# Mixer norm: root applied behind the input projections, squares summed on VectorE, first slabs dealt in another order

## The reference, cut to what matters

```python
x = _layernorm(DN_ALPHA * x + y, ssd_ln_g[j], ssd_ln_b[j])   # "ln2" in the kernel
h = x
a = rmsnorm(h, g_mix[i])                  # h * rsqrt(mean(h*h) + 1e-6) * g_mix; "mix" in the kernel
proj = a @ w_in[i]
cb, cc, cu, q, k, v = jnp.split(proj, splits, axis=-1)       # 512 columns each
conv_out = head_rmsnorm(short_gated_conv(cb, cc, cu, conv_w[i]), g_conv_out[i])   # cb * conv3(cc * cu)
attn = stick_breaking_attention(to_heads(q), to_heads(k), to_heads(v))            # 8 heads of 64
attn = head_rmsnorm(attn..., g_attn_out[i])
h = h + jnp.concatenate([conv_out, attn], axis=-1) @ w_out[i]
```

## Time and profile before

| | |
|---|---|
| median of three runs | 2727.25 us |
| the profiled execution | 2722.69 us |
| its span | 2720.9 us |
| TensorE (PE) busy | 2642.7 us, 97% |
| VectorE (DVE) busy | 1713.4 us, 63% |
| ScalarE (ACT) busy | 938.1 us, 34% |
| GpSimd (POOL) busy | 1150.4 us, 42% |
| from ln2's root to the first v turned | 1372.7 to 1433.0 us |
| the attention loop | about 1436 to 1865 us |

### The profile page before, as it was taken

The page is one execution under the profiler, slowest core; times in us unless marked ns, Lnnn a source line. Parts: engine busy times, 40 slices in busy tenths (PEclk is TensorE's granted clock), DMA queues, the critical chain, the costliest instruction groups (busy, mean ns, idle before and its releaser), DMA issues.

```text
span 2720.9 us, 32191 instructions
## 1 busy us (share of the span) xinstructions
PE 2642.7 (97%) x12394; PEld 2117.3 (78%) x12394; DVE 1713.4 (63%) x2087; ACT 938.1 (34%) x1208; POOL 1150.4 (42%) x1422
## 2 busy tenths in 40 slices
PE   8999999999999999999999999998999999999998
PEld 7877878787887887887767777776888888888886
DVE  6636663778658658758865665666355656555556
ACT  2537880422212211212256666575211111111132
POOL 4633435431431431431421222223555676655653
PEclk9999999999999999999999999999999999999999
DMA  3110003210110110110230000002111111111312
GB/s 135 51 47 32 24 20 109 66 47 24 39 48 23 40 54 16 47 47 16 78 131 24 32 24 32 24 32 85 55 39 55 55 55 55 47 47 54 117 47 78
DMA packets 39937, 139.37 MB, mean 51 GB/s; under 512 B 4400, under 2 KB 4528, under 8 KB 39792
## 3 DMA queue, kind: packets, MB, share of 16 engines
q1 hardware_dynamic: 31392, 110.11, 12.3%
q10 hardware_dynamic: 8400, 27.26, 2.7%
HBM read 124.77 MB, written 12.58 MB: 50 GB/s over the span
## 4 chain that ended last, share of the span: by engine, by line
PE 82%; DVE 11%; ACT 4%; issue 2%; POOL 1%; ACTq 0%; DVEq 0%; POOLq 0%
PE PS L759 37%; PE PS L1437 13%; PE PS L1463 10%; PE PS L996 2%; PE PS L1089 2%; PE PS L1485 2%; PE PS L1130 2%; PE PS L1315 1%; PE PS L895 1%; PE PS L1332 1%; PE PS L909 1%; PE PS L1354 1%; PE PS L1132 1%; PE PS L1036 1%; ACT mla_p L1662 1%
## 5 line engine op out<-in xcount | busy, mean ns | idle before, releaser
L612 POOL CAST w_hi<-w_stage 128x1024 fp32r<-128x1024 f32 x130 | 143.3, 1102 | 1116.7 <-PE PS L759 757.9
L615 POOL TENSOR_TENSOR w_lo<-w_stage,w_hi 128x256 fp32r<-128x256 f32 x520 | 504.2, 1000 | 10.4
L759 PE MATMUL PS<-XH,w_hi 128*128 128x512 f32 x1216 | 384.6, 398 | 7.7 <-DVE XL L2519 2.9
L759 PE MATMUL PS<-XL,w_hi 128*128 128x512 f32 x1216 | 375.9, 390 | 0.0
L759 PE MATMUL PS<-XH,w_lo 128*128 128x512 f32 x1216 | 375.4, 390 | 0.0
L759 PEld LDWEIGHTS PS<-XH,w_hi 128*128 128x128 f32 x1216 | 222.4, 188 | 61.0 <-issue 10.0
L759 PEld LDWEIGHTS PS<-XL,w_hi 128*128 128x128 f32 x1216 | 228.4, 188 | 48.5
L759 PEld LDWEIGHTS PS<-XH,w_lo 128*128 128x128 f32 x1216 | 228.4, 188 | 48.4
L686 POOL TENSOR_TENSOR w_lo<-w_stage,w_hi 128x256 fp32r<-128x256 f32 x260 | 220.3, 854 | 0.0
L682 POOL CAST w_hi<-w_stage 128x256 fp32r<-128x256 f32 x260 | 125.9, 487 | 185.7 <-PE PS L1437 108.3
L1437 PE MATMUL PS<-raw_hi,w_hi 128*128 128x512 f32 x512 | 158.2, 390 | 0.0
(11 more groups left out here) (459 smaller groups left out, 5620.7 us busy)
## 6 DMA issues: line engine op xcount, KB each, us to landing
w_stage<-w SPq DMA_DIRECT2D x202, 512.0 KB, 3.3
H<-x_t ACTq DMA_DIRECT2D x8, 512.0 KB, 8.0
pj_kept<-ple_proj_tiles ACTq DMA_DIRECT2D x8, 512.0 KB, 2.6
h_kept<-H ACTq DMA_DIRECT2D x8, 512.0 KB, 3.5
H<-h_kept ACTq DMA_DIRECT2D x4, 1024.0 KB, 5.0
out_t<-out_tiles SPq DMA_DIRECT2D x16, 256.0 KB, 2.1
x_again<-x_t ACTq DMA_DIRECT2D x12, 256.0 KB, 3.1
ple_proj_a<-pj_kept ACTq DMA_DIRECT2D x1, 2048.0 KB, 9.1
```

The lines of the kernel that those rows point to most:

```text
L612: nc.gpsimd.tensor_copy(w_hi[:, slot, :, :], w_stage[:, slot, :, :]).then_inc(s_w_hi, 1)
L615: nc.gpsimd.tensor_tensor(w_lo[:, slot, k:k + 2, :], w_stage[:, slot, k:k + 2, :], w_hi[:, slot, k:k + 2, :].bitcast(F32), ALU.subtract).t ...
L759: mm = nc.tensor.matmul(outs[:, half, :], wt[:, slot, k, :], a[:, k - first, half * HB:(half + 1) * HB], start=(k == whole[0] and wt is w_ ...
```

## The change

- Mixer norm. ScalarE squares tile k into one of eight buffers of its own (MIX_SQ). It makes XH directly from H with the gain as scale, without the root. VectorE makes XL from H with a `scalar_tensor_tensor`. Scale, shift and low part are interleaved in one pass (`norm_two`). Behind the last low part VectorE adds up the eight squares (seven adds into ACM), and TensorE multiplies the ones matrix with that sum alone, in the middle of slab k.
- The root RM (per token, along the free axis, the same in all partitions) and its square RM2 are made behind the first slabs. `key_roots` also makes RK, the root per token along the partitions, by a product with the identity and a reduce.
- Where the root goes in: z is copied out as z * RK * RM; the exponential weights are multiplied by RK in the high copy (scale) and in the low part; cc * cu is multiplied by RM2 ahead of the first tap; the conv result by RM after the last tap. The output of v needs RK only, hence the weights carry it.
- The order of pieces: projection pieces 6 and 7 come directly after pieces 4 and 5; slabs v and q are dealt by the list MIX_PIECES, then four tiles of k, the ones product, four tiles of k. Slab 2 (k) also starts on its high weights.

```diff
+MIX_PIECES = [0, 0, 1, 0, 1, 0, 1, 0, 0, 1, 0, 0, 1, 1, 1, 1]
...
             proj_piece(5)
-            norm_sums(mix)
             proj_piece(6)
...
-                    if i < 2:
+                    if i < 3:
                         pe.wait_ge(s_w_hi, n + 1)
...
-            for k in range(8):
-                sb_piece(0, k)
-                if 1 <= k <= 5:
-                    sb_piece(1, k - 1)
-            progress[0] = 13
-            sb_pieces(11)
+            done = [0, 0]
+            for i in MIX_PIECES:
+                sb_piece(i, done[i])
+                done[i] += 1
+            progress[0] = 16
+            sb_pieces(4)
+            mix["ss"].wait(pe, KT - 1)
+            for half in range(2):
+                mm = nc.tensor.matmul(PS[:, 2 + half, :], CN[:, C_ONES, :], ACM[:, half * HB:(half + 1) * HB], start=True, stop=True)
+            mm.then_inc(mix["cs"].sem, 1)
+            sb_pieces(4)
+            mix["v"].wait(pe, 1)
             turn_v(0)
...
-                nc.scalar.activation(SQN[:, k % 2, :], TN[:, k % 2, :], ACT.Square, bias=col("ln2_b", k)).then_inc(mix["sq"].sem, 1)
-                if k in (0, 1):
+                nc.scalar.activation(MIX_SQ[k][:, :], TN[:, k % 2, :], ACT.Square, bias=col("ln2_b", k)).then_inc(mix["sq"].sem, 1)
+                if k < 4:
                     proj_copy(4 + k)
+                ln2["h"].wait(act, k + 1)
+                nc.scalar.activation(XH[:, k, :], H[:, k, :], ACT.Copy, scale=col("g_mix", k)).then_inc(mix["hi"].sem, 1)
+                act.dma_start(h_kept[k, :, :], H[:, k, :]).then_inc(s_hk, 16)
+                if k < 4:
                     proj_out(4 + k)
-            norm_root(mix, EPS6)
-            for k in range(KT):
-                norm_hi(mix, k)
...
+            sb_copies(SB_ORDER[0])
+            sb_copies(SB_ORDER[1])
+            nc.scalar.preload_act_table_set("natural_log_exp_and_others")
+            mix["cs"].wait(act, 1)
+            inverse_root(RM[:, :], flat(1), D, EPS6, mix["v"].sem, mix["v"].base, mix["rs"].sem)
+            sb_copies(SB_ORDER[2])
...
-                        nc.scalar.activation(WH[:, T1 % 2, :, q1:HB], a, ACT.Copy).then_inc(s_wh, 1)
+                        j1 = SB_UNITS[step - 1][1]
+                        nc.scalar.activation(WH[:, T1 % 2, :, q1:HB], a, ACT.Copy, scale=RK[:, j1:j1 + 1]).then_inc(s_wh, 1)
...
+                def low(k):
+                    mix["hi"].wait(dve, k + 1)
+                    v.scalar_tensor_tensor(out=XL[:, k, :], in0=H[:, k, :], scalar=col("g_mix", k), in1=XH_f[:, k, :],
+                                           op0=ALU.mult, op1=ALU.subtract).then_inc(mix["lo"].sem, 1)
...
                 for k in range(KT):
                     if k >= 2:
+                        ln2["h"].wait(dve, k - 1)
+                        mix["sq"].wait(dve, k - 1)
+                    v.scalar_tensor_tensor(out=TN[:, k % 2, :], in0=H[:, k, :], scalar=col("ln2_g", k), in1=RS[:, :],
+                                           op0=ALU.mult, op1=ALU.mult).then_inc(ln2["t"].sem, 1)
                     if k:
+                        shifted(k - 1)
+                    if k > 1:
+                        low(k - 2)
+                shifted(KT - 1)
+                low(KT - 2)
+                low(KT - 1)
+                for k in range(1, KT):
+                    mix["sq"].wait(dve, k + 1)
+                    if k > 1:
+                        mix["ss"].wait(dve, k - 1)
+                    v.tensor_tensor(ACM[:, :], MIX_SQ[0][:, :] if k == 1 else ACM[:, :], MIX_SQ[k][:, :], ALU.add).then_inc(mix["ss"].sem, 1)
+
+            def key_roots():
+                mix["rs"].wait(dve, 1)
+                turned = ACM[:, :].rearrange("p (j t) -> p j t", t=P)
+                v.tensor_tensor(turned, RM[:, :].rearrange("p (j t) -> p j t", t=P),
+                                CN[:, C_ID, :].unsqueeze(1).to_broadcast([P, KT, P]), ALU.mult).then_inc(mix["t"].sem, 1)
+                mix["t"].wait(dve, 1)
+                v.tensor_reduce(RK, turned, AX.X, ALU.add).then_inc(mix["t"].sem, 1)
+                mix["t"].wait(dve, 2)
+                v.tensor_tensor(RM2[:, :], RM[:, :], RM[:, :], ALU.mult).then_inc(mix["c"].sem, 1)
...
+                    v.tensor_tensor(CC[:, :], CC[:, :], RM2[:, :], ALU.mult).then_inc(mix["c"].sem, 1)
+                    mix["c"].wait(dve, root_product("cc", m))
                     cc(v.tensor_scalar(y, CC[:, :], col("c2_w", 8 + m), None, ALU.mult))
...
+                    if d == 2:
+                        v.tensor_tensor(y, y, RM[:, :], ALU.mult).then_inc(mix["c"].sem, 1)
...
-                v.tensor_tensor(WL[:, T % 3, :, q0:HB], ZS[:, T % 3, :, q0:HB], WH[:, T % 2, :, q0:HB].bitcast(F32),
-                                ALU.subtract).then_inc(s_wl, 1)
+                v.scalar_tensor_tensor(out=WL[:, T % 3, :, q0:HB], in0=ZS[:, T % 3, :, q0:HB], scalar=RK[:, j:j + 1],
+                                       in1=WH[:, T % 2, :, q0:HB].bitcast(F32), op0=ALU.mult, op1=ALU.subtract).then_inc(s_wl, 1)
...
             sb_lows(("q", 0))
+            key_roots()
             sb_lows(("k", 0))
...
-                        v.tensor_copy(z, PS[:, 0:2, q0:HB]).then_inc(s_zc, 1)
+                        v.scalar_tensor_tensor(out=z, in0=PS[:, 0:2, q0:HB], scalar=RK[:, j:j + 1],
+                                               in1=RM[:, hf * HB + q0:(hf + 1) * HB].unsqueeze(1).to_broadcast([P, 2, HB - q0]),
+                                               op0=ALU.mult, op1=ALU.mult).then_inc(s_zc, 1)
```

More of the change, by code:

```diff
@@ L91, in sb_bank_turn, with cc_step, root_product @@
     return SB_BANK_USE.index(key)
+CC_STEPS = []
+for _m in range(4):
+    for _step in range(SB_STEPS):
+        _cbs = [("cb", k[1], None) for k in sb_finished(_m, _step, 0) if k[0] == "cb"]
+        _taps = [("tap", _m, d) for d in range(3) if _step > d and ("cu", _m) in sb_finished(_m, _step - d - 1, 0)]
+        CC_STEPS += _cbs + _taps if (_m, _step) in HEAD_STEPS else _taps + _cbs
+        CC_STEPS += [("cb", k[1], None) for k in sb_finished(_m, _step, 1) if k[0] == "cb"]
+def cc_step(kind, m, d=None):
+    return CC_STEPS.index((kind, m, d)) + 1
+ROOT_PRODUCTS = ["root"] + [(kind, m) for m in range(4) for kind in ("cc", "y")]
+def root_product(*key):
+    return ROOT_PRODUCTS.index(key) + 1
+MIX_PIECES = [0, 0, 1, 0, 1, 0, 1, 0, 0, 1, 0, 0, 1, 1, 1, 1]
 DT_STEPS = 23
@@ L1289, in sb_piece @@
                         pe.wait_ge(s_bank, sb_bank_turn((kind, m)))
-                mm = product(outs, n, XH, XL, [k], 0, range(8), ready=(mix["lo"].sem, mix["lo"].base) if i == 0 else None, quarters=i < 2)
+                mm = product(outs, n, XH, XL, [k], 0, range(8), ready=(mix["lo"].sem, mix["lo"].base) if i == 0 else None, quarters=i < 3)
                 if k == 7:
@@ L2504, in _, with norm_two @@
             half_low(1, KT - 1)
-            def norm_dve(s, gain, center=None, split=True, keep=False):
-                t = Tally(dve, s["t"].sem, s["t"].base)
-                if center:
-                    c = center
-                    s["cs"].wait(dve, 1)
-                    c(v.tensor_scalar(MU[:, :], flat(2), 1.0 / D, None, ALU.mult)); c.wait()
-                    for k in range(KT):
-                        c(v.tensor_tensor(H[:, k, :], H[:, k, :], MU[:, :], ALU.subtract))
-                s["rs"].wait(dve, 1)
+            def norm_two(c):
+                ln2["cs"].wait(dve, 1)
+                c(v.tensor_scalar(MU[:, :], flat(2), 1.0 / D, None, ALU.mult)); c.wait()
+                for k in range(KT):
+                    c(v.tensor_tensor(H[:, k, :], H[:, k, :], MU[:, :], ALU.subtract))
+                ln2["rs"].wait(dve, 1)
@@ L2521, in shifted @@
                 def shifted(k):
-                    s["t"].wait(dve, k + 1)
-                    v.tensor_scalar(H[:, k, :], TN[:, k % 2, :], col("ln2_b", k), None, ALU.add).then_inc(s["h"].sem, 1)
-                finish = low if split else shifted
+                    ln2["t"].wait(dve, k + 1)
+                    v.tensor_scalar(H[:, k, :], TN[:, k % 2, :], col("ln2_b", k), None, ALU.add).then_inc(ln2["h"].sem, 1)
                 for k in range(KT):
                     if k >= 2:
-                        s["lo" if split else "h"].wait(dve, k - 1)
-                        if not split:
-                            mix["sq"].wait(dve, k - 1)
-                    t(v.scalar_tensor_tensor(out=TN[:, k % 2, :], in0=H[:, k, :], scalar=col(gain, k), in1=RS[:, :],
-                                             op0=ALU.mult, op1=ALU.mult))
-                    if k:
-                        finish(k - 1)
@@ L2788, in _ @@
             out_tiles(N_CORE + 3, GROUPS - 1, centre2)
-            norm_dve(ln2, "ln2_g", center=centre2, split=False, keep=True)
-            norm_dve(mix, "g_mix")
+            norm_two(centre2)
             cc = Tally(dve, s_cc)
```

30 lines of the change are left out of this document (15 added, 15 removed).

## The result

The changed kernel took 2729.8 us (median of its runs) against 2724.45 for the kernel before beside it: a ratio of 1.0016, 95% interval 1.0009 to 1.0022. It is slower, by less than 0.2%, where 0.9975 was forecast. One run of each kernel took twice as long (5567 and 5333 us) and is left out of the ratio. The profiled execution took 2726.88 us with a span of 2725.1.

A forecast was written before the change was run, and what follows sets the result against it. TensorE, busy 97% of the span, was taken as the bound. Front -12.2 us plus loop +5.4 us made -6.8 us: 2715.9 against the profiled execution, 2720.4 us carried over to the median; range 2714 to 2730.

The forecast's parts named there:

- GpSimd's split of slab q: Second norm: cast 1.30 us, low parts 6.60 us; VectorE loses 2.5 us over five instructions beside it.
- the front: Stretch from second norm's root through slab k: k ends at 1420.6 instead of 1432.9, gain 12.2 us.
- TensorE is held by GpSimd's weights: Rival: the front keeps its end, so only the loop's +5.4 us shows, 2732.6 us; chance 0.05.
- The Trainium skill's rule: Splits in the front: VectorE would lose 3.9 us a split, not 2.5; net would be -4.2 us.
- the clock stays at the upper level: Front: TensorE's clock keeps 2.4 GHz through the stretch with waits, as from 1376 to 1404 before.
- the loop cost: Attention loop, 1436 to 1865: 20.6 us added to VectorE and ScalarE together, of which 5.4 us shows.
- VectorE's front: Second norm: scale, shift and low part take 3.23 us a tile; last low part ends at 1401.1.
- The adds: Seven adds of squares end at 1412.8, TensorE wants the sum at 1413.4: no wait, margin 0.6 us.
- VectorE's front queue longer: Rival: contention or late high parts make TensorE wait for the sum; net +0.2, 2727.4 us; chance 0.22.
- the shares named for "faster": Chance 0.56 of measurably faster: two thirds of forecast's cases, nearly all of loop hides, a fifth of long front queue.
- Passing on: Loop: 18 TensorE waits on softplus low parts and low weights pass on the added VectorE and ScalarE time, 2.0 us.
- Products: Loop, two new products per head pair: exposed 1.0 us in pair 0, 0.3 in pairs 1 and 2, 2.1 in last.

The follow-up runs named there:

- e5: The changed kernel unaltered, run again in a later session; 2719.0 us, ratio 0.9973.
- e12: e10's kernel with VectorE waiting for its own low part once, at k = 6; 2724.3 us, ratio 0.9992.
- first trace: Trace of the changed kernel's profiled execution in its first measurement, against the kernel before; 2726.88 us.
- e13: e10's kernel with all eight v tiles ahead of q; 2722.1 us, ratio 0.9991.
- e10: The changed kernel with projection piece 7 moved behind the first v tile; 2729.3 us, ratio 1.0016.
- e4: The changed kernel without the eight convolution products with the root and its square; 2715.8 us, ratio 0.9964.
- e8: The changed kernel unaltered once more, on one chip with the kernel with gaps; 2718.8 us, ratio 0.9976.
- the first study: First measurement of the changed kernel beside the kernel before; 2729.8 us, ratio 1.0016.
- e2: The changed kernel with VectorE waiting for its own low part at k = 4 alone; 2718.9 us, ratio 0.9974.
- e6: The changed kernel with the column root left out of the weights' high and low parts; 2714.8 us, ratio 0.9958.
- e7: The changed kernel with z copied plainly, without both roots; 2716.1 us, ratio 0.9963.
- the late variants: The changed kernel with projection piece 7 behind the first v tile (e10 to e13) or the second (e14); 2719.8 to 2729.3 us.
- The kernel with gaps: The changed kernel with e1's waits, run in two sessions; 2719.5 and 2718.7 us, ratio 0.9978 both times.
- e11: e10's kernel with VectorE waiting for its own low part in every tile; 2719.8 us, ratio 0.9976.
- e14: The changed kernel with projection piece 7 behind the second v tile; 2720.0 us, ratio 0.9978.
- e1: The changed kernel with VectorE waiting for its own low part in every tile from the third on; 2719.5 us, ratio 0.9978.

## Why the prediction was wrong

**The step that failed** is the one on GpSimd's split of slab q: "There its cast took 1.30 and its low parts 6.60 us ... Over the five VectorE instructions beside that split I put the loss at 2.5 us". It took for granted who loses: a cast of GpSimd was to come in within 1.30 us and VectorE was to be stretched for it. That was read off the only overlap in the trace of before, and there each scale, from the third on, waited on the semaphore of the low part just ahead, which left 0.03 us between them (1396.74 to 1396.77). The change took these waits out: a scale now waits for a shift that lies two instructions back. I counted this as a gain of VectorE and did not ask whom the gaps had served. With VectorE's instructions touching, the cast lost all its boundaries for 13.8 us (14.83 - 1.04). VectorE lost 0.45 us in the same time (the last low part, 1.73). TensorE stood for 12.23 us behind the cast, where the prediction had no wait for it, and the front gained 2.6 us and not 12.2.

**The rival that came true** was "TensorE is held by GpSimd's weights", given 0.05 and +5.4 us (2732.6). Measured: 2729.8. The argument against it, the split times of before, was the failed step again.

**The Trainium skill's rule**, page "SBUF — State Buffer", section "SBUF: two separate sides" (an exclusive port pair, and the loser blocks for the whole instruction), was weighed with the wrong loser too: I let VectorE lose and came to a net of -4.2 us. The traces of e5 and e12 agree with its exclusive lock (the cast that got in stretched the scale from 1.28 to 1.94 in e12, and the shift from 0.75 to 1.53 in e5). The first trace adds what bears on the time here: the loser went on losing at 13 boundaries in a row.

**How the wait became time.** e13 shows it: not the cast's delay, but the order written for TensorE, in which q's first tile stands third. I had praised this order for keeping TensorE in work; with a late cast it does the reverse. The slow clock behind the idle stretch, which I had not forecast ("the clock stays at the upper level"), is part of the bill: the first pairs of matmuls behind the wait took 1.22 and 1.05 us instead of 0.62.

A second dip of the clock is not tied to the cast. In pair 0 of the loop a wait of 1.59 us is followed by a pair of 1.08 us in the first trace (clock 0.53 over the next 3 us) and of 0.73 in e5 (clock 1.00). Pair 0 took 110.6 and 110.7 us in the two traces with this dip alone (the first and e10), 111.2 in e13 with a dip behind an earlier wait, 110.9 in e4 with both dips and without the products, and 109.7 in e5, e8 and, with the cast kept out, e12. So the same program went both ways, and I can't say what decides.

**Where the cast is let in, the forecast stands.** In e5 the front gained 12.1 us (12.2 forecast) and the loop cost 5.5 (5.4); in e8 it was 12.1 and 6.1. The ratios of e5 and e8, 0.9973 and 0.9976, are the one forecast (2720.4/2727.25 = 0.9975). In detail:
- VectorE's front: the last low part ends 28.8 us behind the root (29.4 forecast). The pitch of an undisturbed tile is 3.06 us, not 3.23 (scale, shift and low part start to start 1.20, 0.66 and 1.20: instructions that don't wait overlap by 0.08), and the splits cost 2.3 us more than in the first trace, where there were none beside it (26.5).
- The adds end 40.1 us behind the root (41.2 forecast), and TensorE wants the sum at 41.9: margin 1.8 and not 0.6. No wait, as said. "VectorE's front queue longer" did not come.
- key_roots ran 1427.16 to 1430.90 in the first trace, across k's high copy at 1430.37, and held k's low part by nothing that shows. Hidden, as costed.
- Two slips of reckoning change nothing: 1432.9 less 1420.6 is 12.3 and not 12.2, and the shares named for "faster" add up to some 0.53 and not 0.56.

**The loop.** VectorE's busy time between the landmarks grew by 15.5 us (306.7 - 291.2; 15.8 forecast), ScalarE's by 4.4 (4.8). The forms cost what the nearest rows had: z 1279 ns against 1218, low weights 1314 against 1275, high weights 1139 against 1046. Passing on: weights 1.4 and z 0.9, 2.3 where 2.0 was forecast. Products in pair 3: 1.1 (2.1 forecast); in pairs 1 and 2: 0 (0.3); in pair 0: 1.3 (1.0), all of it in the step from the eighth to the ninth copy of z, where TensorE has a new wait of 0.92 us for low weights (1489.89 in the first trace) that e4 lacks. Pair 0 grew by 2.0 us in e5. Most of what the product doesn't explain lies from the tenth to the eleventh copy of z (9.20 us before, 10.33 in e5, 10.20 in e4 without products), and I can't give its cause. The terms read from the traces make 2.3 + 1.3 + 0 + 1.1 = 4.7 of the 5.5 us measured. So the sum of the loop was right to 0.1 us partly by luck: the last pair was put 1.0 too high, and a cost of some 0.8 was not in it.

**What stays open.** Why gapless VectorE keeps the cast out in some programs and runs (the first study, e10, e12, e13) and lets it in at the first boundary in others (e2 to e8), with the same 0.22 us of phase in the first trace and in e5 (and in e6 and e7). All runs of one kernel in one session lay on one side: all of the first study at 2726.9 or above, 9 and 9 later at 2722.2 or below. So for this kernel it was not drawn anew in each execution. Chip and session changed together, so these runs can't part the two. The phase in the shift (0.16 us let in, 0.37 to 0.41 kept out) fits the late variants, but the two traces of the unaltered kernel speak against phase as the whole answer. The kernel with gaps was not run in a session in which the unaltered kernel was kept out, and e10 was not run beside e11 to e14.

**The safer version,** as far as the runs go, is the changed kernel with the wait of e1: 2719.5 and 2718.7 us (0.9978 both times). It is faster than before by 0.22% on two chips, and its late form on a third (0.9976). Where the plain changed kernel is let in, it is as fast (2719.0 and 2718.8). That the gaps cure a session in which it is kept out is argued from e12 and not shown; no trace with gaps in every tile was kept out.

## What to carry to other kernels

A price read off an overlap holds only for the rhythm in which it was read: ask which waits made the gaps that let the other engine in, and whether the change keeps them. When VectorE runs back to back on SBUF, don't put work that hangs on a GpSimd instruction at the head of another engine's order; give GpSimd a gap (0.03 us was enough in e12), or order the other engine so that it has work until VectorE is done. And when a kernel's first measurement misses a forecast, measure the same kernel again in another session before explaining.

## What the runs showed of the hardware

- A cast of 1.04 us on GpSimd took 14.83, 13.45, 13.45 and 8.58 us beside VectorE instructions with SBUF operands that touched, while these kept their 1.28 and 0.75 us. It got in at the first gap in VectorE each time, 0.24, 0.24, 0.24 and 0.03 us wide (first trace, e10, e13, e12), and ended 0.9 us after the VectorE instruction ahead of the gap, as did the cast of before, at its gap of 0.03 us.
- The same program had two levels, 2729.8 us in one session, 2719.0 and 2718.8 in two others, each held by all its runs of the session.
- VectorE instructions that wait for nothing overlap: a scale of 1.28 us is followed after 1.20, a shift of 0.75 after 0.66 (first trace, 1378.89 to 1380.75). Behind a wait on the instruction ahead the start is 0.03 us after its end (before, 1396.74 to 1396.77; e12, 1395.27 to 1395.30).
